# Modulated blocks of an encoder kernel: written in place in their PSUM bank instead of copied to a buffer in SBUF

## Chip, core and metric

The kernel runs on one core of one Trainium2 chip. The metric is the device time of one execution in microseconds. A core has TensorE (PE), VectorE (DVE), ScalarE (ACT), GpSimd (POOL) and SyncE (SP), which run their own instruction streams and wait for each other on semaphores.

## What is computed

Two layers of an encoder run over 1024 prompt rows and 256 sample rows of width 1024. Each layer normalizes its rows, scales and shifts them per channel (the modulation), runs a mixer (latent attention beside a spatial gating group, joined in an output projection), adds the result, normalizes and modulates again and runs a feed-forward part with 2816 hidden channels:

```
h = rmsnorm(x, g_pre_mix) * (1 + sc1) + sh1
x = x + ga1 * rmsnorm(mixer(h), g_post_mix)
h = rmsnorm(x, g_pre_ffn) * (1 + sc2) + sh2
f = (silu(h @ w_gate) * (h @ w_up)) @ w_down
x = x + ga2 * rmsnorm(f, g_post_ffn)
```

The scale and shift columns differ between prompt and sample rows. All inputs and outputs are float32.

## The kernel before

Rows are held as ten tiles of 128 rows, `tokm`. Matrix products run on pairs of values: a high half, rounded to the format that TensorE takes, and a low half, the rest. Each product is three matmuls (`product`, lines 595 to 597): high by low, low by high and high by high. So every input of a product has to be transposed into channel-major order and split into `ht_hi` and `ht_lo`.

One modulated block is one 128-channel slice k of one group of row tiles. A group has 512 or 256 rows in the mixer (`GROUPS`), and 512, 128, 384 or 256 rows in the feed-forward part (`FFN_GROUPS`). There are 112 such blocks. Each goes through this chain:

- TensorE transposes the row tiles of the group, one 128x128 transpose for each, into PSUM bank 6 or 7 (`transposes`, lines 599 to 607). The number n of a block is its place among all users of these two banks, and the bank is 6 + n % 2. Before the transposes TensorE waits until block n - 2 has been read out of the bank: on `s_tbm`, when that block is a modulated one, and otherwise on `s_ht`.
- ScalarE scales and shifts the bank into one of two slots of `tbank` in SBUF (`modulated_bank`, lines 929 to 935). It waits for the transposes and, on `s_ht`, until VectorE is through with block n - 2, whose slot it takes. It then counts `s_tbm` up.
- VectorE waits for `s_tbm`, casts the slot to `ht_hi`, waits for its own cast (`link`), subtracts `ht_hi` from the slot to form `ht_lo`, and counts `s_ht` up (`split_bank`, lines 1351 to 1358).
- TensorE's products of a group wait on `s_ht` until all eight blocks of the group are split.

The same two banks serve the gained blocks (keys "lora" and "out"): there ScalarE writes `ht_hi` from the bank (`gained_bank`, line 947), and VectorE forms `ht_lo` from the bank and `ht_hi` in line 1369.

The order of work is written out by hand and is the same list on every engine: `z_order` for the input products of a layer, `out_order` for the output projection, `AHEAD` and `NEXT_AHEAD` for blocks that are sent ahead within the feed-forward loops. All instructions of an engine run in the order of these lists. Places with modulated blocks are:

- the first run: in layer 0, eight blocks of 512 columns before the first input product;
- pairs of blocks between input products in layer 0, and of the last group in layer 1;
- the start of layer 1: four blocks of 512 columns before its first input product, then four and four blocks of the second group around one product;
- the output projection: two blocks behind each of the products of row tiles 5 to 8, and eight blocks of 128 columns behind tile 8, before the product of tile 9. Behind tiles 5 and 6 gained blocks of the last group follow through the same banks;
- the feed-forward part: eight blocks in a row (four of 384 and four of 256 columns) at the start of its second half, and single blocks or pairs within its loops.

GpSimd splits the weights into `w_hi` and `w_lo` (lines 580 and 582), and SP loads them. Residuals are added on VectorE (lines 1378 and 1380) after ScalarE has formed a sum of squares (line 896). The buffer `tbank` also carries bias rows of the modulation in its first two partitions.

Of the kernel before, what the change touches and what calls it, by code (L numbers as in the profile page):

```python
# [18 lines left out]
F32 = mybir.dt.float32  # L19
F32R = mybir.dt.float32r  # L20
ALU = mybir.AluOpType
ACT = mybir.ActivationFunctionType
AX = mybir.AxisListType

P = 128
# [8 lines left out]
def trunk_program(nc, a, y_prompt, y_sample):  # L34
# [41 lines left out]
    with ctx:  # L76
        ctx.enter_context(nc.allow_non_contiguous_dma(reason="columns of gains, modulation and spatial bias, one element per partition"))

        def sb(name, shape, dt=F32):
            return ctx.enter_context(nc.sbuf_tensor(name, shape, dt))  # L80

        def sem(name):
            return ctx.enter_context(nc.semaphore(name))


        ht_hi = sb("ht_hi", [P, KT, TOK], F32R)
# [8 lines left out]
        tbank = sb("tbank", [P, 2, HB])  # L95
# [9 lines left out]
        ps = ctx.enter_context(nc.psum_tensor("ps", [P, 8, HB], F32))  # L105
# [100 lines left out]
        def w_block(b, kt, n):  # L206
            return [w[:, (b % 2) * HALF_RING:(b % 2) * HALF_RING + kt * n].rearrange("p (k n) -> p k n", n=n) for w in (w_hi, w_lo)]
# [5 lines left out]
        plan, uses, lin, tb_no, tb_keys = {}, [0] * 8, [0], {}, []  # L213
# [181 lines left out]
        s_tbm = sem("bank_modulated")  # L395
        s_ht = sem("ht_ready")
# [61 lines left out]
        def after_product(eng, key):  # L458

            b, n = plan[key]  # L460
            eng.wait_ge(rdy[b], n + 1)
            return b
# [123 lines left out]
        def _(pe):  # L586
            def bank(key):
                b, n = plan[key]
                if n:
                    pe.wait_ge(fre[b], n)  # L590
                return b
# [7 lines left out]
            def transposes(key, srcs):  # L599
                b, n = plan[key][0], tb_no.get(key, 0)  # L600
                if n >= 2:

                    last = tb_keys[n - 2][0]
                    pe.wait_ge(s_tbm if last in ("mix", "ffn") else s_ht, n - 1)
                for i, src in enumerate(srcs):
                    ins = pe.transpose(ps[:, b, i * P:(i + 1) * P], src, ident[:, :])  # L606
                ins.then_inc(rdy[b], 1)
# [7 lines left out]
            for n, key in enumerate(FIRST_MOD):  # L615
                key = ("mod",) + key
                pe.wait_ge(s_wm[n % 2], 32 * (n // 2 + 1))
                b = bank(key)
# [4 lines left out]
            for l in range(L):  # L623

                for e in z_order(l):
                    if e[0] == "tb":
                        _, gi, k = e
                        t0, nt = GROUPS[gi]
                        if k == 0:
                            pe.wait_ge(s_xn, xn_count(l, 0) + t0 + nt)  # L630
                        transposes(("mix", l, gi, k), [row_block(t0 + i, k) for i in range(nt)])
                    else:
                        _, c, t = e
                        n = Z[c][1] - Z[c][0]
                        if c == 0:
                            pe.wait_ge(s_ht, ht_count("mix", l, group_of(t)))
                        b = bank(("z", l, c, t))
                        w = w_block(c, KT, n)
                        for k in range(KT):
                            if t == 0:  # L640
                                pe.wait_ge(s_w, last_piece[(l, c, k)])
                            ins = product(ps[:, b, 0:n], act_cols(t, k), [x[:, k, :] for x in w], k == 0, k == KT - 1)
                        ins.then_inc(rdy[b], 1)

                pe.wait_ge(s_wsl, 16 * (l + 1))
                for i in range(2):
                    transposes(("wsp", l, i), [stage[:, g * P:(g + 1) * P] for g in range(4 * i, 4 * i + 4)])
                pe.wait_ge(s_wsr, 2 * (l + 1))
                for gi, (t0, nt) in enumerate(GROUPS):
                    pe.wait_ge(s_vn, l * NT + t0 + nt)  # L650
                    for bb in range(4):
                        b = bank(("sgu", l, gi, bb))
# [5 lines left out]
                for e in lora_order:  # L658
                    if e[0] == "tb":
                        _, gi, k = e  # L660
                        t0, nt = GROUPS[gi]
# [3 lines left out]
                    else:  # L665
                        t = e[1]
                        pe.wait_ge(s_ht, ht_count("lora", l, group_of(t)))
                        for c in range(4):
                            b = bank(("qkv", l, t, c))
                            blk, kt, k0, n = (4, QKT, 0, H * QK) if c < 2 else (5, KVT, QKT, H * (NOPE + VD))  # L670
                            w = w_block(blk, kt, n)
# [139 lines left out]
                for e in out_order:  # L811
                    if e[0] == "tb":
                        _, gi, k = e
                        t0, nt = GROUPS[gi]
# [7 lines left out]
                    else:  # L822
                        t = e[1]
                        pe.wait_ge(s_ht, ht_count("out", l, group_of(t)))
                        for c in range(2):
                            w = w_block(6 + c, KT, HB)
                            b = bank(("outp", l, t, c))
# [56 lines left out]
        def _(act):  # L884
# [42 lines left out]
                act.dma_start(cols[:, PRE0:PRE0 + KT], a[("g_pre_mix", "g_pre_ffn")[which]][l].rearrange("(k p) -> p k", p=P)).then_inc(s_cols, 16)  # L927

            def modulated_bank(key, groups, gi, scale, shift):
                n = tb_no[key]  # L930
                b = after_product(act, key)
                if n >= 2:
                    act.wait_ge(s_ht, n - 1)
                w = groups[gi][1] * P
                act.activation(tbank[:, n % 2, 0:w], ps[:, b, 0:w], ACT.Identity, bias=shift, scale=scale).then_inc(s_tbm, 1)  # L935

            def modulated_row_bank(key):
                gi, k = key[-2:]
                groups = FFN_GROUPS[key[2]] if key[0] == "ffn" else GROUPS
                g = mod_group(groups[gi][0])  # L940
                modulated_bank(key, groups, gi, c_scale(g, k), c_shift(g, k))
# [51 lines left out]
            for l in range(L):  # L993
# [11 lines left out]
                for n, e in enumerate(z_order(l)):  # L1005
# [6 lines left out]
                    if e[0] == "tb":  # L1012
                        _, gi, k = e
                        g = mod_group(GROUPS[gi][0])
                        modulated_bank(("mix", l, gi, k), GROUPS, gi, c_scale(g, k), c_shift(g, k))
                        continue
                    _, c, t = e
                    b = after_product(act, ("z", l, c, t))
                    if c < 2:
                        n, sq, o = ((QL, QL, ST_Q), (KVR, KVL, ST_KV))[c]  # L1020
# [15 lines left out]
                for i in range(2):  # L1036
                    b = after_product(act, ("wsp", l, i))
# [21 lines left out]
                for e in lora_order:  # L1059
                    if e == ("qkv", TP):  # L1060
                        load_first(0, TP, s_first_prompt)
                    if e[0] == "tb":
                        _, gi, k = e
# [4 lines left out]
                    else:  # L1068
# [5 lines left out]
                        for c in range(2):  # L1074
                            b = after_product(act, ("qkv", l, t, 2 + c))
# [149 lines left out]
                for e in out_order:  # L1225
                    if e[0] == "tb":
                        _, gi, k = e
# [5 lines left out]
                    else:  # L1233
# [12 lines left out]
                        for c in range(2):  # L1246
                            b = after_product(act, ("outp", l, t, c))
# [58 lines left out]
        def _(dve):  # L1306
            chain = [0]

            def link(ins):

                chain[0] += 1
                ins.then_inc(s_dve, 1)
                dve.wait_ge(s_dve, chain[0])
# [19 lines left out]
            for n, key in enumerate(FIRST_MOD):  # L1333
                if n < 2:
                    first_rows(n)
                key = ("mod",) + key
                b = after_product(dve, key)
# [13 lines left out]
            def split_bank(key, groups, gi, k):  # L1351
                n = tb_no[key]
                t0, nt = groups[gi]
                hi, lo = (h[:, k, t0 * P:(t0 + nt) * P] for h in (ht_hi, ht_lo))
                dve.wait_ge(s_tbm, n + 1)
                src = tbank[:, n % 2, 0:nt * P]
                link(dve.tensor_copy(hi, src))  # L1357
                dve.tensor_tensor(lo, src, hi.bitcast(F32), ALU.subtract).then_inc(s_ht, 1)  # L1358

            def split_row_bank(key):  # L1360
                gi, k = key[-2:]
# [43 lines left out]
            for l in range(L):  # L1405
                if l == 0:
                    form_cols(l, 0)
                for n, e in enumerate(z_order(l)):
# [7 lines left out]
                    if e[0] == "tb":  # L1416
                        _, gi, k = e
# [11 lines left out]
                for i in range(2):  # L1429
                    b = plan[("wsp", l, i)][0]  # L1430
                    dve.wait_ge(s_wsh, 2 * l + i + 1)
                    hi, lo = (w[:, 4 * i:4 * i + 4, :].rearrange("p g t -> p (g t)") for w in wsp)
# [59 lines left out]
                for e in lora_order:  # L1492
                    if e[0] == "tb":
                        _, gi, k = e
                        gained_low(("lora", l, gi, k), gi, k, cols[:, GAIN0 + k:GAIN0 + k + 1])
                    else:
# [11 lines left out]
                        for c in range(2):  # L1508
                            b = after_product(dve, ("qkv", l, t, c))
# [120 lines left out]
                for e in out_order:  # L1630
                    if e[0] == "tb":
                        _, gi, k = e
# [110 lines left out]
```

## Time and profile before

| | |
|---|---|
| time, median of 3 runs | 3699.86 us (3693.75 to 3711.45) |
| time of the profiled execution | 3690.44 us |
| span of the profiled execution | 3688.6 us |
| mean granted TensorE clock | 0.958 of 2.4 GHz |
| PE busy | 3356.2 us (91%) |
| DVE busy | 1583.4 us (43%) |
| ACT busy | 1031.6 us (28%) |
| POOL busy | 1396.3 us (38%) |

The span is the time from the first to the last instruction of the core. Busy time counts the instructions of an engine without its waits. All times of single instructions come from this one profiled execution.

### The profile page before, as it was taken

Reading aid. Unit: us, or ns where it says so; the run is one execution under the profiler, and the core shown is the slowest. Engines: PE = TensorE matmul, PEld = TensorE weight load, DVE = VectorE, ACT = ScalarE, POOL = GpSimd, SP = SyncE. Lnnn points to the kernel's source line nnn. Section 1 sums busy time; section 2 is a strip of 40 time slices with the busy share of each in tenths; the row PEclk is TensorE's granted clock in tenths of the full one; section 3 lists DMA queues with packets and bytes.
Section 4 is the critical chain, followed back from the end, with each engine's and each line's share of the span. In section 5 each row is a group of like instructions: output and inputs, shape, how many; then the busy total and the mean of one; then the engine's idle time right before and its main releaser. Section 6 shows DMA issues by size and latency. Waiting matters only on the chain. (4 is left out here: it accounts for less than half of the span.)

```text
span 3688.6 us, 48829 instructions
## 1 busy us (share of the span) xinstructions
PE 3356.2 (91%) x19532; PEld 3022.7 (82%) x19532; DVE 1583.4 (43%) x2807; ACT 1031.6 (28%) x2298; POOL 1396.3 (38%) x804
## 2 busy tenths in 40 slices
PE   5997888888999999899988978887999999999996
PEld 2987777767899998889988767776789999899996
DVE  3115777764333333433333146887333333352223
ACT  2323455553200101210014234777330011121001
POOL 2210577830544454445540302000045444455441
PEclk7998999989999999999999988998999999999998
DMA  6205554432322223322223134111232222233221
GB/s 209 69 20 151 144 157 134 147 100 75 123 78 75 69 80 80 110 80 76 79 68 102 57 113 136 26 38 55 81 120 75 75 75 69 86 120 92 80 75 63
DMA packets 397728, 337.90 MB, mean 92 GB/s; under 512 B 107192, under 2 KB 325000, under 8 KB 397504
## 3 DMA queue, kind: packets, MB, share of 16 engines
q1 hardware_dynamic: 249808, 233.18, 20.7%
q10 hardware_dynamic: 147696, 101.61, 9.4%
q8 instruction: 156, 2.56, 0.3%
q14 instruction: 68, 0.56, 0.0%
HBM read 282.87 MB, written 51.87 MB: 91 GB/s over the span
## 5 line engine op out<-in xcount | busy, mean ns | idle before, releaser
L580 POOL TENSOR_SCALAR w_hi<-raw 128x1024 fp32r<-128x1024 f32 (+2 forms) x400 | 438.1, 1095 | 2183.9 <-PE ps L597 2051.7
L582 POOL TENSOR_TENSOR w_lo<-raw,w_hi 128x1024 fp32r<-128x1024 f32 (+2 forms) x400 | 965.9, 2415 | 33.3
L595 PE MATMUL ps<-ht_lo,w_hi 128*128 128x320 f32 x2816 | 874.1, 310 | 4.9 <-DVE ht_lo L1358 3.0
L596 PE MATMUL ps<-ht_hi,w_lo 128*128 128x320 f32 x2816 | 872.4, 310 | 0.0
L597 PE MATMUL ps<-ht_hi,w_hi 128*128 128x320 f32 x2816 | 872.3, 310 | 0.0
L595 PE MATMUL ps<-w_lo,ht_hi 128*128 128x512 f32 (+2 forms) x2040 | 785.6, 385 | 60.4 <-DVE ht_lo L1358 22.5
L596 PE MATMUL ps<-w_hi,ht_lo 128*128 128x512 f32 (+2 forms) x2040 | 778.5, 382 | 0.0
L597 PE MATMUL ps<-w_hi,ht_hi 128*128 128x512 f32 (+2 forms) x2040 | 777.1, 381 | 0.0
L595 PEld LDWEIGHTS ps<-ht_lo,w_hi 128*128 128x128 f32 x2816 | 530.7, 188 | 8.1 <-DVE ht_lo L1358 3.8
L596 PEld LDWEIGHTS ps<-ht_hi,w_lo 128*128 128x128 f32 x2816 | 530.8, 188 | 1.6
L597 PEld LDWEIGHTS ps<-ht_hi,w_hi 128*128 128x128 f32 x2816 | 530.6, 188 | 0.0
L595 PEld LDWEIGHTS ps<-w_lo,ht_hi 128*128 128x128 f32 x2040 | 393.1, 193 | 130.9 <-DVE ht_lo L1358 24.1
L597 PEld LDWEIGHTS ps<-w_hi,ht_hi 128*128 128x128 f32 x2040 | 392.5, 192 | 65.5
L596 PEld LDWEIGHTS ps<-w_hi,ht_lo 128*128 128x128 f32 x2040 | 393.2, 193 | 61.7
L1667 DVE TENSOR_TENSOR ps<-ps,stage 128x320 f32<-128x320 f32 x176 | 87.8, 499 | 823.1 <-PE ps L597 814.5
L1683 DVE TENSOR_TENSOR tokm<-ps,tokm 128x512 f32<-128x512 f32 x400 | 275.8, 690 | 246.8 <-PE ps L597 246.8
L1271 ACT ACTIVATE stage<-ps 128x320 f32<-128x320 f32 x176 | 75.6, 437 | 924.6 <-PE ps L597 915.9
L1278 ACT ACTIVATE ht_hi<-ps 128x320 fp32r<-128x320 f32 x176 | 77.0, 438 | 560.7 <-DVE ps L1667 560.7
L606 PE MATMUL ps<-ident,tokm 128*128 128x128 f32 x580 | 107.4, 322 | 102.0 <-ACT tbank L935 47.5
L1547 DVE TENSOR_TENSOR ht_lo<-ps,ht_hi 128x512 fp32r<-128x512 f32 (+1 forms) x288 | 177.9, 653 | 37.8 <-ACT ht_hi L1148 36.6
L1536 DVE TENSOR_REDUCE stat<-ps 128x1 f32<-128x1024 f32 (+1 forms) x160 | 169.0, 1056 | 49.4 <-PE ps L597 49.0
L606 PEld LDWEIGHTS ps<-ident,tokm 128*128 128x128 f32 x580 | 78.9, 162 | 127.5 <-ACT tbank L935 36.9
(127 smaller groups left out, 3690.4 us busy)
## 6 DMA issues: line engine op xcount, KB each, us to landing
raw<-in_w_gate_dram SPq DMA_DIRECT2D x88, 512.0 KB, 3.8
raw<-in_w_up_dram SPq DMA_DIRECT2D x88, 512.0 KB, 3.8
raw<-in_w_down_dram SPq DMA_DIRECT2D x88, 512.0 KB, 3.5
raw<-in_w_mod_dram SPq DMA_DIRECT2D x80, 512.0 KB, 4.1
x_rows<-tokm ACTq DMA_DIRECT2D x30, 512.0 KB, 5.0
x_old<-x_rows ACTq DMA_DIRECT2D x30, 512.0 KB, 4.3
kv_rows<-stage ACTq DMA_DIRECT2D x20, 512.0 KB, 3.3
tokm<-kv_rows ACTq DMA_DIRECT2D x30, 320.0 KB, 4.2
```

The costliest lines, as they stand in the source:

```text
L580: pool.tensor_scalar(hi, r, 1.0, 0.0, ALU.mult, ALU.add).then_inc(s_whi, 1)
L582: pool.tensor_tensor(lo, r, hi.bitcast(F32), ALU.subtract).then_inc(s_w, 1)
L595: pe.matmul(out, lhs[0], rhs[1], start=first, stop=False)
L596: pe.matmul(out, lhs[1], rhs[0], start=False, stop=False)
L597: return pe.matmul(out, lhs[0], rhs[0], start=False, stop=last)
L606: ins = pe.transpose(ps[:, b, i * P:(i + 1) * P], src, ident[:, :])
L1271: act.activation(stage[:, c * 320:(c + 1) * 320], ps[:, c, 0:320], ACT.Silu).then_inc(s_sil, 1)
L1278: act.activation(act_ring(half, j % 4)[0][:, c * 320:(c + 1) * 320], ps[:, 2 + c, 0:320], ACT.Copy).then_inc(s_ah, 1)
L1536: link(dve.tensor_reduce(c, psf[:, (u % 2) * 1024:(u % 2) * 1024 + w], AX.X, ALU.max))
L1547: dve.tensor_tensor(lo, ps[:, 4 + c, 0:w * P].rearrange("p (k q) -> p k q", q=P), hi.bitcast(F32), ALU.subtract).then_inc(s_ptl, 1)
L1667: dve.tensor_tensor(up, up, stage[:, c * 320:(c + 1) * 320], ALU.mult).then_inc(s_a32, 1)
L1683: dve.tensor_tensor(f, ps[:, 4 + n % 2, :], f, ALU.add).then_inc(s_acc, 1)
```

## The change

A modulated block is no longer copied to `tbank`. ScalarE reads the bank twice: the first activation writes the high half straight to `ht_hi`, the second writes the scaled and shifted values back into the same bank. VectorE then subtracts `ht_hi` from the bank and writes `ht_lo`; its cast and the wait behind the cast are gone. ScalarE no longer waits for `s_ht`. TensorE waits on `s_ht` for block n - 2 before it writes a bank, whatever kind of block that was.

```diff
             def transposes(key, srcs):
                 b, n = plan[key][0], tb_no.get(key, 0)
                 if n >= 2:
-
-                    last = tb_keys[n - 2][0]
-                    pe.wait_ge(s_tbm if last in ("mix", "ffn") else s_ht, n - 1)
+                    pe.wait_ge(s_ht, n - 1)
...
             def modulated_bank(key, groups, gi, scale, shift):
-                n = tb_no[key]
-                b = after_product(act, key)
-                if n >= 2:
-                    act.wait_ge(s_ht, n - 1)
-                w = groups[gi][1] * P
-                act.activation(tbank[:, n % 2, 0:w], ps[:, b, 0:w], ACT.Identity, bias=shift, scale=scale).then_inc(s_tbm, 1)
+                t0, nt = groups[gi]
+                rows = ps[:, after_product(act, key), 0:nt * P]
+                act.activation(ht_hi[:, key[-1], t0 * P:(t0 + nt) * P], rows, ACT.Identity, bias=shift, scale=scale)
+                act.activation(rows, rows, ACT.Identity, bias=shift, scale=scale).then_inc(s_tbm, 1)
...
                 dve.wait_ge(s_tbm, n + 1)
-                src = tbank[:, n % 2, 0:nt * P]
-                link(dve.tensor_copy(hi, src))
-                dve.tensor_tensor(lo, src, hi.bitcast(F32), ALU.subtract).then_inc(s_ht, 1)
+                dve.tensor_tensor(lo, ps[:, plan[key][0], 0:nt * P], hi.bitcast(F32), ALU.subtract).then_inc(s_ht, 1)
```

## Rows read from the trace of the kernel before

**Rows 1.** The page, part 1: busy time, share of the span, instructions.

```profile
PE 3356.2 (91%) x19532; PEld 3022.7 (82%) x19532; DVE 1583.4 (43%) x2807; ACT 1031.6 (28%) x2298; POOL 1396.3 (38%) x804
```

**Rows 2.** The view of waits: us in total, times, longest us.

```profile
PE ps L606 <- ACT tbank L935: 47.5, 35, 17.1
...
PE ps L595 <- DVE ht_lo L1358: 25.5, 8, 7.3
```

**Rows 3.** Groups by line and form: busy us, mean ns, idle before.

```profile
L935 ACT ACTIVATE tbank<-ps,cols 128x512 f32<-128x512 f32 x48 | 35.7, 775 | 65.1 <-DVE cols L1348 24.2 <-DVE ht_lo L1358 17.5 <-issue 16.4
L935 ACT ACTIVATE tbank<-ps,cols 128x128 f32<-128x128 f32 x16 | 7.3, 457 | 3.9 <-DVE ht_lo L1358 2.6 <-PE ps L606 1.3
L1022 ACT ACTIVATE ps<-ps 128x384 f32<-128x384 f32 x20 | 9.5, 475 | 0.6
L1547 DVE TENSOR_TENSOR ht_lo<-ps,ht_hi 128x512 fp32r<-128x512 f32 x256 | 164.5, 683 | 29.9 <-ACT ht_hi L1148 28.8
```

**Rows 4.** Three lines of VectorE: duration min/median/max in ns, first and last start.

```profile
L1357 DVE CAST ht_hi<-tbank x112: 220/420/2500, 64.7 to 3195.2; 128x512 fp32r<-128x512 f32 x48, 128x256 fp32r<-128x256 f32 x32, 128x128 fp32r<-128x128 f32 x16, 128x384 fp32r<-128x384 f32 x16
L1358 DVE TENSOR_TENSOR ht_lo<-tbank,ht_hi x112: 292/691/2373, 65.2 to 3195.6; 128x512 fp32r<-128x512 f32 x48, 128x256 fp32r<-128x256 f32 x32, 128x128 fp32r<-128x128 f32 x16, 128x384 fp32r<-128x384 f32 x16
L1673 DVE TENSOR_TENSOR ht_lo<-ps,ht_hi x176: 491/492/494, 978.3 to 3645.9; 128x320 fp32r<-128x320 f32 x176
```

**Rows 5.** The timeline, first run: start us, us, instruction, idle before it.

```profile
63.89 1.45 ACT L935 ACTIVATE tbank<-ps,cols 128x512 f32<-128x512 f32 x2 [24.21 <-DVE cols L1348]
65.16 2.18 DVE L1358 TENSOR_TENSOR ht_lo<-tbank,ht_hi 128x512 fp32r<-128x512 f32 x1
68.27 1.12 PE L606 MATMUL ps<-ident,tokm 128*128 128x128 f32 x4 [1.58 <-ACT tbank L935]
83.29 0.69 PE L595 MATMUL ps<-w_lo,ht_hi 128*128 128x384 f32 x1 [3.82 <-DVE ht_lo L1358]
```

**Rows 6.** The timeline, start of layer 1.

```profile
1927.87 1.45 ACT L935 ACTIVATE tbank<-ps,cols 128x512 f32<-128x512 f32 x2 [16.38 <-issue]
1937.33 0.69 PE L595 MATMUL ps<-w_lo,ht_hi 128*128 128x384 f32 x1 [7.31 <-DVE ht_lo L1358]
```

**Rows 7.** The timeline, second token group of layer 1.

```profile
1969.70 1.63 ACT L935 ACTIVATE tbank<-ps,cols 128x512 f32<-128x512 f32 x2 [0.63 <-PE ps L606]
1972.15 0.59 PE L595 MATMUL ps<-w_lo,ht_hi 128*128 128x288 f32 x1
1976.86 1.45 ACT L935 ACTIVATE tbank<-ps,cols 128x512 f32<-128x512 f32 x2
1982.06 0.69 PE L595 MATMUL ps<-w_lo,ht_hi 128*128 128x384 f32 x1 [3.05 <-DVE ht_lo L1358]
```

**Rows 8.** The timeline, last pair of the second token group of layer 0.

```profile
119.01 1.45 ACT L935 ACTIVATE tbank<-ps,cols 128x512 f32<-128x512 f32 x2
122.09 0.44 PE L595 MATMUL ps<-w_lo,ht_hi 128*128 128x384 f32 x1 [3.12 <-DVE ht_lo L1358]
```

**Rows 9.** The timeline, second half of the feed-forward part of layer 0.

```profile
1430.45 1.23 ACT L935 ACTIVATE tbank<-ps,cols 128x384 f32<-128x384 f32 x2 [15.23 <-DVE tokm L1683]
1437.67 0.64 PE L595 MATMUL ps<-ht_lo,w_hi 128*128 128x320 f32 x1 [1.48 <-DVE ht_lo L1358]
```

**Rows 10.** The timeline, output projection of layer 1.

```profile
2657.32 1.45 ACT L935 ACTIVATE tbank<-ps,cols 128x512 f32<-128x512 f32 x2
2660.89 0.41 PE L606 MATMUL ps<-ident,tokm 128*128 128x128 f32 x2 [1.63 <-DVE ht_lo L1369]
...
2693.08 1.28 DVE L1378 SCALAR_TENSOR_TENSOR tokm<-tokm,stat,gate_row 128x1024 f32<-128x1024 f32 x1
...
2704.55 1.45 ACT L935 ACTIVATE tbank<-ps,cols 128x512 f32<-128x512 f32 x2 [2.88 <-DVE gate_row L1387]
...
2710.62 0.45 PE L606 MATMUL ps<-ident,tokm 128*128 128x128 f32 x1 [0.23 <-ACT tbank L935]
```

**Rows 11.** Busy time by stretch: us, PE, PEld, DVE, ACT, POOL busy, PEclk, DMA.

```profile
122.00:127.00 5.00, 4.91 (x19) 4.91 (x20) 0.03 (x1) 0.00 (x0) 0.00 (x0) 0.66 0.02 3
145.00:150.00 5.00, 4.95 (x28) 4.95 (x29) 0.00 (x0) 0.48 (x1) 0.00 (x0) 1.00 0.01 3
```

## The prediction

> **What bounds the kernel now.** I read the page first. TensorE is busy 91% of the span, ScalarE and VectorE far less [rows 1], so work on those two counts only where TensorE stands still for it. The view of waits prices that: TensorE stood 47.5 us in front of transposes until `tbank` was written and 25.5 us in front of products until `ht_lo` was written [rows 2]. The 112 modulated blocks are worth at most these 73 us, 2% of the span. From the timeline I then took each stretch where one of those waits ends last. The 20 blocks sent ahead within the feed-forward loops have their whole chain beside TensorE's work, and I cost them at nothing; their cover is the tiles of gate and up products, and were it gone, one more activation each would cost 20 x 0.67 = 13 us.
>
> **What one block costs before and after.** Before, a 512-column block takes on ScalarE 0.775 us (two in a row 1.45 us, so the second starts 0.67 us after the first) [rows 3, 5], on VectorE a cast (0.42 us) and a subtract (0.69 us; both medians over all sizes) [rows 4]. The same two stretch to 2.5 and 2.37 us at worst [rows 4]; the first run has a subtract of 2.18 us [rows 5], with GpSimd splitting weights beside it.
>
> After, ScalarE issues two activations from one bank. The first has the old one's operands, so it keeps 0.775 us. The second writes the bank in place with pointer scale and bias. The nearest row for a write in place is the square of line 1022, 0.475 us for 384 columns with constant operands; by column it would be about 0.58 us at 512 [rows 3]. I take 0.775 us, since scale and bias are the same kind as in line 935, and keep 0.58 us as the lower end. So a block holds its bank 1.45 us on ScalarE, and ScalarE is free after 1.34 us. VectorE loses the cast and its wait on itself, and the subtract reads the bank: line 1547 does this at 512 columns in 0.683 us [rows 3]. Beside GpSimd: line 1673 has the same operands with a bank as first source and takes 491 to 494 ns in all 176 cases between 978 and 3646 us [rows 4], and GpSimd is busy 38% of the span [rows 1], so many of them stood beside it. So I take 0.69 us, never stretched; upper end 2.2 us.
>
> The Trainium skill speaks against the move here: its page VectorE: DVE Perf Modes, section on the TRN2 errata, charges a VectorE instruction 120 cycles from PSUM and 58 from SBUF, 65 ns more per subtract. The rows above say no such thing (0.683 against 0.691 us). By the page some 33 subtracts on the path would add an estimated 2 us, and the forecast below would be 3710.5 us.
>
> The waits move too. ScalarE no longer waits for `s_ht`; TensorE's next transpose into a bank waits for the subtract of two blocks before instead of the activation. Queued behind that wait stand all of TensorE's later products. A bank's round is now: transposes T, activations 1.45, subtract 0.69, three handovers, for every second block. For a handover I take 0.04 us (the pair of [rows 8] lasts 3.08 us with 3.0 us of instructions in it and five handovers). T is 1.12 us in the first run [rows 5], and about half of that at full clock.
>
> **The sum, place by place.**
>
> First run, layer 0. ScalarE starts at 63.89, products at 83.29 [rows 5]. After: the second block is subtracted at 63.89 + 0.67 x 2 + 1.45 + 0.72 = 67.4; three more rounds of 1.12 + 1.45 + 0.69 + 0.12 = 3.38 end at 77.5. **Gain 5.8 us.**
>
> Start of layer 1, four blocks. Start 1927.87, products at 1937.33 [rows 6]. Second block done at 1931.4, one round of 0.56 + 1.45 + 0.69 + 0.12 = 2.8 more: 1934.2. **Gain 3.1.** The residual work behind it hangs on the next product, and shifts with it.
>
> Layer 1, second token group: four blocks from 1969.70, then a product that began at 1972.15, four blocks from 1976.86, products at 1982.06 [rows 7]. After: the fourth block's transposes wait for the second's subtract, 1969.70 + 2.79 + 0.72 = 1973.2, and end at 1973.8, so the product is 1.65 late. The next four start at 1978.5; second block done at 1982.0, one more round 1984.85. **Loss 2.8.**
>
> Pairs between products. Before, the last pair went from 119.01 to 122.09 [rows 8]; after, 2.79 + 0.72 = 3.5 us instead of 3.1: 0.5 with a small wait for a bank, 0.6. Two more last pairs, of 256 columns, by the same rule 0.4 each. **Loss 1.4.**
>
> Second half of the feed-forward, once a layer: four blocks of 384 columns, four of 256; start 1430.45, products at 1437.67; the pair of 1.23 us gives a step of 0.56 [rows 9]. After: second block done at 1430.45 + 1.12 + 1.23 + 0.6 = 1433.4, a round of 384 columns 2.3, two of 256 columns 1.95 each: 1439.7. **Loss 2.1, twice.**
>
> Output projection, once a layer. Behind the sixth product two modulated blocks and three gained blocks go through the same two banks; the last gained transposes ran at 2660.89 [rows 10]. After: the second subtract ends at 2657.32 + 2.79 + 0.72 = 2660.83, and the gained subtract behind it takes 0.44 more: 0.45 lost; the same behind the seventh. Behind the eighth the residual of line 1378 waited at 2693.08 for the sum of squares that ScalarE runs after two blocks: 1.3 later, and with it the gate row and the blocks at 2704.55 [rows 10]. There two blocks of 512 and eight of 128 columns stand; a 128-column activation is 0.457 us [rows 3], two about 0.82. After: the eighth 512-column block is done at 2705.85 + 2.79 + 0.72 = 2709.4, three rounds of some 1.6 and a transpose end at 2714.6, where the last transpose ended at 2711.07 [rows 10]. So 3.6 with the 1.3. **Loss 4.5, twice.**
>
> Sum: -5.8 - 3.1 + 2.8 + 1.4 + 4.2 + 9.0 = **+8.5 us**. The profiled execution took 3690.44 us (span 3688.6), which makes 3698.9; it lies 9.4 below the median of the runs, 3699.86. Against the median I say **3708.4 us**, 0.23% more. No DMA and no step on SP's or GpSimd's queue is added or moved. With the in-place activation at 0.58 us some 28 rounds on the path each save 0.19 us: 3703.
>
> **The rivals.**
>
> *The clock (slower).* After the 3.12 us gap at 122.09 TensorE was granted 0.66 of 2.4 GHz over 5 us, part of it at 1.2 GHz; after the next shorter gap 1.00 [rows 8, 11]. The first cost 5 x 0.34 = 1.7 us. The losses above lengthen eight gaps: two (256-column ends) would newly fall to 1.2 GHz, six would stay there that much longer. It decides if a gap longer by 0.4 to 3.6 us buys one more such stretch: 8 x 1.7 = 13.6, 3722 us. For it: these gaps all grow. Against: a grown gap may only move the same stretch.
>
> *The subtract from the bank is stretched by GpSimd after all.* Then both gains go: 3717 us. Against it stands line 1673 [rows 4].
>
> *The second activation nearly free (faster).* Were it overlapped with the first, the 28 rounds of 0.67 us fall away: -19, so 3690 us; the sign turns at about 0.37 us each. Against: two successive activations overlap only 0.1 us [rows 3, 5].
>
> *Covered on both sides:* the longer chains meet waits that I did not see, on DMA or on the residuals, and gains and losses mostly vanish: 3700 us.
>
> **Numbers.** About 0.5% (18.5 us) is what a measurement of this kernel can tell from no change. Chances: forecast 0.55, clock 0.20, stretched subtract 0.05, nearly free 0.10, covered 0.10. Of these over 0.5% slower: nearly all of the clock case, half of the stretched one, and a tail of the forecast, 0.23; over 0.5% faster only the far end of the fast case, 0.05; the rest 0.72. The range goes from 3694, inside the fast case with the runs' own scatter, to 3723, which takes in the clock case.
>
> **What would show it.** After, the first run should end near 77.5 us, with no subtract of line 1352 above 0.7 us; ScalarE's in-place activation should read about 0.78 us at 512 columns; the stop before the ninth-tile products of each layer should grow by some 3.6 us, and TensorE's waits in front of transposes should name the subtract, not ScalarE. The forecast is wrong if in-place activations read under 0.4 us, if the subtracts in the first run exceed 1 us, or if the granted clock after these gaps drops clearly further than before.

## The result, and the profile after

The changed kernel takes **3716.66 us** (median, 3706.77 to 3722.09) against 3699.86 us before: a ratio of 1.0042, 95% interval 1.0028 to 1.0056, so 15.5 us slower (10.4 to 20.7). The forecast was 8.5 us more, 3708.4 us: the time lies in its range of 3694 to 3723 us, but the interval leaves 8.5 us out. Line numbers of the kernel after: L930 is the activation into `ht_hi`, L931 the one in place, L1352 the subtract from the bank, L604 the transposes; the products stay in L595 to L597.

Part 1 of the page, after, answers to [rows 1]:

```profile
PE 3369.6 (91%) x19532; PEld 3032.2 (82%) x19532; DVE 1475.8 (40%) x2695; ACT 1089.6 (29%) x2410; POOL 1386.8 (37%) x804
```

VectorE lost 108 us of work and ScalarE gained 58, yet the kernel is slower: neither was the bound. The groups by line and form, after, to be held against [rows 3]:

```profile
L930 ACT ACTIVATE ht_hi<-ps,cols 128x512 fp32r<-128x512 f32 x48 | 37.3, 777 | 53.2 <-DVE cols L1344 23.5 <-issue 16.3 <-DVE gate_row L1381 8.6
...
L931 ACT ACTIVATE ps<-ps,cols 128x512 f32<-128x512 f32 x48 | 35.9, 748 | 0.0
...
L1352 DVE TENSOR_TENSOR ht_lo<-ps,ht_hi 128x512 fp32r<-128x512 f32 x48 | 33.2, 691 | 72.4 <-ACT ps L931 72.4
```

The in-place activation costs 748 ns against 777 for the other: the 0.775 us taken for it was right, the 0.58 us of the lower end was not. The line L1352 over the whole span, min/median/max in ns:

```profile
L1352 DVE TENSOR_TENSOR ht_lo<-ps,ht_hi x112: 291/558/693, 64.2 to 3218.8; 128x512 fp32r<-128x512 f32 x48, 128x256 fp32r<-128x256 f32 x32, 128x128 fp32r<-128x128 f32 x16, 128x384 fp32r<-128x384 f32 x16
```

No subtract takes over 693 ns, where [rows 4] had 2373, and 29 of the 112 had GpSimd at work beside them for nine tenths of their time or more. The Trainium skill's figure (page VectorE: DVE Perf Modes, the TRN2 errata section: 120 cycles from PSUM, 58 from SBUF) would set this subtract an estimated 65 ns above the old one. It takes 691 ns at 512 columns, and in the kernel before the 37 subtracts of that size without GpSimd beside them took 691 to 694, so the measurement does not bear the figure out here. The view of waits, after, answers to [rows 2]:

```profile
PE ps L604 <- DVE ht_lo L1352: 69.7, 46, 17.6
...
PE ps L595 <- DVE ht_lo L1352: 19.0, 8, 3.4
```

TensorE's wait for ScalarE (47.5 us before) is gone, and one for VectorE's subtract of 69.7 us has come; the wait of the products fell from 25.5 to 19.0 us. In sum that is 88.7 against 73.0, of which TensorE's wait for the subtract of gained blocks gives some back (24.0 us before, 16.7 after). The chain moved from two engines that overlapped into one bank that is held until all is done.

The timeline of the first run, after, against [rows 5]:

```profile
62.79 0.78 ACT L930 ACTIVATE ht_hi<-ps,cols 128x512 fp32r<-128x512 f32 x1 [23.52 <-DVE cols L1344]
63.47 0.74 ACT L931 ACTIVATE ps<-ps,cols 128x512 f32<-128x512 f32 x1
64.13 0.78 ACT L930 ACTIVATE ht_hi<-ps,cols 128x512 fp32r<-128x512 f32 x1
64.24 0.69 DVE L1352 TENSOR_TENSOR ht_lo<-ps,ht_hi 128x512 fp32r<-128x512 f32 x1 [1.49 <-ACT ps L931]
...
64.99 1.11 PE L604 MATMUL ps<-ident,tokm 128*128 128x128 f32 x4 [17.59 <-DVE ht_lo L1352]
...
65.58 0.69 DVE L1352 TENSOR_TENSOR ht_lo<-ps,ht_hi 128x512 fp32r<-128x512 f32 x1 [0.65 <-ACT ps L931]
66.14 0.78 ACT L930 ACTIVATE ht_hi<-ps,cols 128x512 fp32r<-128x512 f32 x1 [0.59 <-PE ps L604]
...
76.38 0.69 PE L595 MATMUL ps<-w_lo,ht_hi 128*128 128x384 f32 x1 [2.24 <-DVE ht_lo L1352]
```

The bank of the first block is free for transposes at 64.99, after both activations and the subtract, and ScalarE's third block starts at 66.14: a round of 3.35 us for two blocks, and products 13.59 us after the first activation instead of 19.40. The same shape without GpSimd beside it is the second half of the feed-forward, after, against [rows 9]:

```profile
1435.82 0.67 ACT L930 ACTIVATE ht_hi<-ps,cols 128x384 fp32r<-128x384 f32 x1 [15.22 <-DVE tokm L1677]
...
1438.18 0.56 DVE L1352 TENSOR_TENSOR ht_lo<-ps,ht_hi 128x384 fp32r<-128x384 f32 x1 [0.57 <-ACT ps L931]
...
1439.56 0.56 DVE L1352 TENSOR_TENSOR ht_lo<-ps,ht_hi 128x384 fp32r<-128x384 f32 x1 [0.82 <-ACT ps L931]
...
1440.27 0.66 PE L604 MATMUL ps<-ident,tokm 128*128 128x128 f32 x2 [0.86 <-DVE ht_lo L1352]
...
1440.68 0.56 DVE L1352 TENSOR_TENSOR ht_lo<-ps,ht_hi 128x384 fp32r<-128x384 f32 x1 [0.57 <-ACT ps L931]
...
1443.12 0.42 DVE L1352 TENSOR_TENSOR ht_lo<-ps,ht_hi 128x256 fp32r<-128x256 f32 x1 [0.70 <-ACT ps L931]
...
1445.41 0.42 DVE L1352 TENSOR_TENSOR ht_lo<-ps,ht_hi 128x256 fp32r<-128x256 f32 x1 [0.70 <-ACT ps L931]
...
1445.89 0.63 PE L595 MATMUL ps<-ht_lo,w_hi 128*128 128x320 f32 x1 [1.54 <-DVE ht_lo L1352]
```

Here the products come 10.07 us after the first activation, before 7.22. Measured in the same way in every place (from ScalarE's first activation of the place to the first product that TensorE runs behind the transposes of its last block), in us:

| Place | before | after | difference | forecast |
|---|---|---|---|---|
| first run | 19.40 | 13.59 | -5.81 | -5.8 |
| start of layer 1 | 9.46 | 6.89 | -2.57 | -3.1 |
| second group of layer 1, both halves | 7.65 | 10.73 | +3.08 | +2.8 |
| three last pairs | 7.21 | 8.36 | +1.15 | +1.4 |
| feed-forward second half, layers 0 and 1 | 14.44 | 20.48 | +6.04 | +4.2 |
| output projection: behind the 6th and 7th product, before the last, both layers | 27.33 | 34.79 | +7.46 | +6.4 |
| the residual ahead of its last blocks, both layers | 55.89 | 58.79 | +2.90 | +2.6 |
| sum | | | **+12.25** | **+8.5** |

The 6.4 and 2.6 are the forecast's 4.5 twice, with its 1.3 for the residual apart. The residual's row runs from the start of the eighth product to ScalarE's first block before the last product, and repeats less well than the others: it read 0.35 us longer per layer in a second profile of the kernel before, and 0.7 in a kernel that leaves this part as it was (the first experiment). The measured 12.25 lies inside the interval of 10.4 to 20.7 us. It is good to 1 or 2 us: between the second profiles of the two kernels (experiments 8 and 9) the same sum is 10.8, mostly because the first run of the kernel before took 20.83 us there.

The term that the forecast put at nothing held: from the product behind the last stop of the output projection to the second half of the feed-forward part, the stretch with 16 of the 20 blocks sent ahead, 478.6 and 478.1 us became 479.4 and 478.0.

### The profile page after: what moved, and what is told of

It reads as the page before. It is cut to its first block and busy times, and to the rows that moved or that the text cites. A ratio compares the mean times of both kernels' runs of the same rounds, so it can differ in the third digit from the quotient of the medians.

```text
span 3712.2 us, 48724 instructions
## 1 busy us (share of the span) xinstructions
PE 3369.6 (91%) x19532; PEld 3032.2 (82%) x19532; DVE 1475.8 (40%) x2695; ACT 1089.6 (29%) x2410; POOL 1386.8 (37%) x804
## 5 line engine op out<-in xcount | busy, mean ns | idle before, releaser
L595 PE MATMUL ps<-ht_lo,w_hi 128*128 128x320 f32 x2816 | 873.7, 310 | 5.0 <-DVE ht_lo L1352 3.1
L597 PE MATMUL ps<-ht_hi,w_hi 128*128 128x320 f32 x2816 | 872.0, 310 | 0.0
L595 PE MATMUL ps<-w_lo,ht_hi 128*128 128x512 f32 (+2 forms) x2040 | 789.7, 387 | 54.0 <-DVE ht_lo L1352 16.0
L597 PE MATMUL ps<-w_hi,ht_hi 128*128 128x512 f32 (+2 forms) x2040 | 780.6, 383 | 0.0
L595 PEld LDWEIGHTS ps<-ht_lo,w_hi 128*128 128x128 f32 x2816 | 530.5, 188 | 8.2 <-DVE ht_lo L1352 3.9
L597 PEld LDWEIGHTS ps<-ht_hi,w_hi 128*128 128x128 f32 x2816 | 530.2, 188 | 0.0
L595 PEld LDWEIGHTS ps<-w_lo,ht_hi 128*128 128x128 f32 x2040 | 395.9, 194 | 125.1 <-DVE ht_lo L1352 17.7
L597 PEld LDWEIGHTS ps<-w_hi,ht_hi 128*128 128x128 f32 x2040 | 394.9, 194 | 65.9
L604 PE MATMUL ps<-ident,tokm 128*128 128x128 f32 x580 | 110.9, 328 | 116.8 <-DVE ht_lo L1352 69.7
L604 PEld LDWEIGHTS ps<-ident,tokm 128*128 128x128 f32 x580 | 80.3, 165 | 143.9 <-issue 47.0
```

Source lines behind the costliest of these rows:

```text
L595: pe.matmul(out, lhs[0], rhs[1], start=first, stop=False)
L597: return pe.matmul(out, lhs[0], rhs[0], start=False, stop=last)
```

## The experiments

Theory: the cost is the longer hold of a bank (two activations and the subtract, in series), place by place; the gain is the subtracts no longer stretched by GpSimd; both add up. First rival: the granted clock behind longer gaps is a large part. Second: the loss is not where the chain says.

**1 and 2. The change at the two places that win, and at all others.** In `modulated_bank`, `split_bank` and `transposes`, chosen by key:

```
+ def in_place(key): return key[:3] == ("mix", 0, 0) or key[:3] == ("mix", 1, 0) and key[3] < 4
...
- last = tb_keys[n - 2][0]
- pe.wait_ge(s_tbm if last in ("mix", "ffn") else s_ht, n - 1)
+ last = tb_keys[n - 2]
+ pe.wait_ge(s_tbm if last[0] in ("mix", "ffn") and not in_place(last) else s_ht, n - 1)
```

`modulated_bank` and `split_bank` take the new code where `in_place(key)` holds and the old code elsewhere. The second kernel has `not (...)` in `in_place`.

> The new scheme only for the first run of layer 0 (eight blocks) and the first four blocks of layer 1, the two places where GpSimd splits weights beside the blocks; the old scheme, with tbank, for the other 100 blocks. By the sum of the prediction: 5.8 + 3.1 = 8.9 us less than before, about 3691 us. If the longer time of the whole change comes from the lost clock behind longer gaps, nothing of it is left here, so again 3688 to 3692 us. Rival, that the stretched casts and subtracts cost TensorE nothing in the end because a later wait takes it back: no change, 3700 us.

> The complement: the old scheme at those two places, the new one for the other 100 blocks. By the sum alone 17.4 us more than before, 3717 us. If the places add up and the whole change costs 16.8 us as measured, this must cost 16.8 + 8.9 = 25.7 us, 3726 us. Rival, that the two gains are taken back later: as the whole change, 3717 us, with the first run back at 19.4 us.

Two places: 3691.13 us, ratio 0.9977 (0.9967 to 0.9987), 8.5 us faster; its places sum to 8.5 us less than before, with the residual 7.0. So the gains are not taken back later. The others: 3719.63 us, 1.0060 (1.0045 to 1.0074), 22 us slower (17 to 27); their places sum to 19.1 us more, with the residual 23. The interval holds both 17.4 and 25.7 of the expectation. So the parts add up within it, and the change is two kernels in one: one that wins where GpSimd works beside VectorE, one that loses elsewhere. In the profile before, GpSimd is busy 15.08 of the 19.3 us from 64.0 and 8.81 of the 11.4 us from 1926.0 (the start of layer 1, with casts of up to 2.22 us and subtracts of up to 1.28), and not at all in the other places of the table. That GpSimd does it is shown for the first run (experiment 11); for the start of layer 1 it is read from the profile.

**3. Without the second activation.** The low halves are then formed from a bank without scale and shift.

```
- act.activation(ht_hi[...], rows, ACT.Identity, bias=shift, scale=scale)
+ act.activation(ht_hi[...], rows, ACT.Identity, bias=shift, scale=scale).then_inc(s_tbm, 1)
- act.activation(rows, rows, ACT.Identity, bias=shift, scale=scale).then_inc(s_tbm, 1)
```

> The whole change without its second activation: ScalarE writes only the high half, and VectorE subtracts it from the bank as the transposes left it, so the low halves hold the wrong values and the computation of the scale and shift is left out of them. The moved wait and the subtract from the bank stay. By the chains of the prediction (rounds shorter by 0.67 us at 512 columns): 20 us less than before, 3680 us, and 28 less than the sum for the change. If lost clock is part of the cost, 40 us less than the change as measured, 3677 us. Rival, that the second activation overlaps and the moved wait is what costs: near the change, 3710 to 3717 us.

3680.29 us, 0.9948 (0.9934 to 0.9962). In its waits the subtract keeps TensorE 21 us less than after the change in front of transposes:

```profile
PE ps L604 <- DVE ht_lo L1351: 48.6, 38, 17.1
...
PE ps L595 <- DVE ht_lo L1351: 13.3, 8, 2.2
```

The second activation is worth some 35 us (0.9948 against 1.0042), of which the places and the residual show 29.8. With it left out, 10 of the 15 places measured are shorter than before, and the other five only 0.2 to 0.7 us longer. The time is the 3680 us of the chains; the 3677 us with lost clock lies inside the interval too.

**4. The wait alone, in the kernel before.**

```
- pe.wait_ge(s_tbm if last in ("mix", "ffn") else s_ht, n - 1)
+ pe.wait_ge(s_ht, n - 1)
```

> The kernel before with one part of the change alone: TensorE waits for the subtract of block n - 2 (s_ht) in front of every transpose into a bank, whatever kind of block it was. Then transpose and activation no longer lie beside the cast and subtract of the block two before. By the rounds at the open places (0.4 us for two blocks of 128 columns, 0.4 for 384, 0.5 for 512; none in the two stretched places, where VectorE sets the pace): about 8 us more than before, 3708 us. If lost clock comes on top, up to 3712 us. Rival, that the wait is covered by the transposes' distance: 3700 us.

3711.27 us, 1.0035 (1.0021 to 1.0050), 13 us slower (8 to 18), more than the 8 us expected; its places sum to 12.5, of which 1.2 is the first run's scatter. The view of waits of this kernel:

```profile
PE ps L605 <- DVE ht_lo L1357: 72.8, 46, 20.4
```

That is as much as after the change (69.7), with the old cast, the old buffer and no second activation: in the bank's round the cast and its waits stand where the second activation stands after the change. With one activation and the subtract in the round the whole ran faster than before (experiment 3); with a third step between them, be it the second activation or the cast, it ran slower.

**5. TensorE kept busy in the stops.** The change, with transposes of the identity into a bank that the next product overwrites, between the blocks of the feed-forward second half (shown) and of the last row tile (36, then 4 each). As the fillers of the second half write bank 0, TensorE also waits there until ScalarE has read that bank:

```
+ def warm(b, count):
+     for _ in range(count):
+         pe.transpose(ps[:, b, 0:P], ident[:, :], ident[:, :])
...
+ if gi == k == 0: pe.wait_ge(s_sil, 2 * (tile_no(l, 1, 0) - 1) + 1)
  transpose_ffn(("ffn", l, 1, gi, k))
+ if (gi, k) == (0, 1): warm(0, 12)
+ elif (gi, k) != (0, 0) and (gi, k) != (1, 3): warm(0, 4)
```

> The changed kernel with transposes of the identity put into TensorE's gaps at four places, into a bank that the next product overwrites: the second half of the feed-forward part (12 behind the first two blocks, 4 behind each later one) and the eight blocks of 128 columns before the last row tile of the output projection (36, then 4 each), in both layers. If granted clock lost behind these gaps is part of the cost, transposes and the first products there run at 2.4 GHz: about 12 us less than the change, 3705 us, and some 20 us less at 1.2 GHz in sum. If clock is no part of it, or the fillers do not hold it: 3717 us or a few us more, since fillers can stand in the way of the next transposes.

3703.78 us, 1.0015 (1.0003 to 1.0027), some 10 us less than the change. The rows below give a stretch, its length, TensorE's busy time, the granted clock as a share of 2.4 GHz, and the share and GB/s of transfers. They are the stop of layer 0's second half and the two stretches of 5 us behind it, for the kernel before:

```profile
1430.45:1437.67 7.22, 3.43 (x15) 0.72 0.00 0
```

```profile
1437.70:1442.70 5.00, 5.00 (x19) 0.50 0.61 5
1442.70:1447.70 5.00, 5.00 (x32) 0.88 0.78 165
```

the same for the changed kernel (138.80 is another place, taken up further down):

```profile
1435.80:1445.90 10.10, 3.69 (x15) 0.71 0.00 0
```

```profile
138.80:143.80 5.00, 5.00 (x20) 0.66 0.00 0
1445.90:1450.90 5.00, 5.00 (x21) 0.57 0.59 4
1450.90:1455.90 5.00, 5.00 (x36) 1.00 0.75 132
```

and for the kernel kept busy, the stop in the last line:

```profile
1442.30:1447.30 5.00, 5.00 (x24) 0.66 0.61 5
1447.30:1452.30 5.00, 5.00 (x36) 1.00 0.81 172
1432.70:1442.20 9.50, 6.04 (x45) 1.00 0.01 2
```

Kept busy, TensorE runs the stop at 1.00, and the stop itself is 9.57 us, not 10.07: its pairs of transposes take 0.41 us, not the 0.66 that they took at 0.50, which is 1.2 GHz. Behind it 1.7 us are lost to the lower clock (5 x 0.34), against 2.1 after the change and 3.1 before. So the fillers win back clock that the kernel before was losing too, and not all of the 10 us is a price of the change. What the change adds in clock behind the stops is small: counted in this way over 10 us behind ten of the places, the kernel before loses 18.4 us in each of two profiles, the changed one 19.4 and 20.5.

**6 and 7. Which version is best?** The two-place kernel with such fillers in all four kinds of places, and then with none in the first run and at the start of layer 1. At the ends they are fewer than in experiment 5: 5, then 3 each in the feed-forward half, and 20, then 2 each before the last row tile. The lines that the second of the two kernels lacks:

```
  transposes(("mix", l, gi, k), ...)
...
- if k == 1: warm(bank(("z", l, 0, 0)), 44 if l == 0 else 12)
- elif 1 < k < last: warm(plan[("z", l, 0, 0)][0], 2 if l == 0 else 5)
```

> The kernel of the two places (new scheme in the first run and at the start of layer 1 alone), with such fillers at the same four places and also in those two runs (44 and 12 behind the first two blocks, 2 and 5 behind later ones). Against 3691 us without fillers, if the clock holds: about 4 less in the first run, 2 at the start of layer 1, 6 in the feed-forward halves, 3 in the output projections: 3676 us. If clock is not to be had so: 3691 us or more.

> The kernel of the two places (in-place scheme in the first run and at the start of layer 1 only) with identity transposes between its blocks at the feed-forward second halves and before the last row tile, and none in the first run or at the start of layer 1. If the fillers buy time only where the next products would have run at 1.2 GHz, the stretches behind these stops lose some 1.5 us each in four places and the median is about 6 us below the two-place kernel without fillers, near 3685 us (against 3691). If what they buy is given back in the attention stretch of layer 0, as the profile of the run with fillers everywhere suggests, the median is again 3690 to 3692 us and that stretch reads about 767 us in its profile against 752.

Everywhere: 3690.91 us, 0.9978 (0.9967 to 0.9989), a miss: no better than two places alone. At the ends only: **3683.57 us, 0.9960 (0.9946 to 0.9974)**, the best of the versions that compute the whole, some 30 us under the change (0.9960 against 1.0042). Its stop and the stretches behind it read

```profile
1436.00:1441.00 5.00, 5.00 (x24) 0.66 0.48 7
1441.00:1446.00 5.00, 5.00 (x36) 1.00 0.55 67
1428.70:1435.90 7.20, 4.59 (x34) 1.00 0.00 0
```

as in experiment 5, and its places have the two-place kernel's lengths within 0.2 us but for one of 0.5 (second group of layer 1), so its gain lies behind the stops. There it is seen: the long stretches from three of the four filled stops to the next place are 1.5, 1.5 and 1.6 us shorter than in the two-place kernel, and counted as above the clock loses 13.8 us over the ten places, where the two-place kernel loses 19.6. The two ratios' intervals (0.9946 to 0.9974 and 0.9967 to 0.9987) just touch.

**8 to 10. Second profiles**, of the kernel before, of the change and of the kernel with fillers everywhere, each unchanged.

> The kernel before, unchanged, profiled a second time: how much of a difference between two profiles belongs to the execution. If executions differ in the attention stretches, the time from the last pair of layer 0 to the blocks behind row tile 6 (751.6 us in the first profile) comes out 3 to 10 us longer, the same stretch of layer 1 (639.1 us) 1 to 4 us longer, while each place with modulated blocks repeats within 0.3 us; the span is then 3693 to 3703 us. If the first profile is typical, both stretches repeat within 1 us and the span is 3688 to 3690 us.

> The changed kernel, unchanged, profiled a second time. If the places make the change, each of them repeats within 0.4 us of its first profile (13.6 us the first run, 10.1 us the feed-forward second half, 8.95 us before the last row tile) whatever the span does; the attention stretch of layer 0 (757.3 us) may move by several us. If instead the change itself slows attention (about 6 us more than before), that stretch reads 757 us again and the kernel before repeats its 751.6 us.

> The two-place kernel with fillers in all four kinds of places, profiled a second time. If the 767.3 us of the attention stretch of layer 0 (753.9 without fillers) was that execution's alone, it reads 752 to 760 us and the span is about 3680 us. If the fillers cause it, by sending TensorE into attention at another moment, it reads 765 to 770 us again and the span is about 3692 us.

| us | before | again | change | again | fillers everywhere | again | fillers at the ends |
|---|---|---|---|---|---|---|---|
| first run | 19.40 | 20.83 | 13.59 | 13.60 | 13.13 | 13.09 | 13.60 |
| feed-forward second half, layer 0 | 7.22 | 7.22 | 10.06 | 10.07 | 7.21 | 7.22 | 7.22 |
| last tile, layer 0 | 6.19 | 6.19 | 8.95 | 8.95 | 6.28 | 6.45 | 6.39 |
| attention stretch, layer 0 | 751.6 | 750.9 | 757.3 | 751.9 | 767.3 | 763.6 | 758.4 |
| attention stretch, layer 1 | 639.1 | 641.2 | 641.7 | 645.4 | 641.2 | 642.5 | 640.6 |

An attention stretch runs from the product behind a layer's last pair to the first activation of its output projection's blocks. The places repeat to 0.2 us, but for the first run of the kernel before, where the stretched subtracts vary (two other kernels with the old chain there, experiments 2 and 4, read 20.70 and 20.56), and for the start of layer 1 with fillers everywhere (6.89 and 6.43). The attention stretches do not: they move by 5 us in layer 0 and 4 in layer 1 between two executions of the changed kernel, while of the kernel before only the one of layer 1 moved, by 2, and its span of 3690.6 us lies between the two readings. So the 5.7 us by which attention looked slower after the change is no part of it that these runs can show, though its two stretches together were 5 to 8 us longer than before in both pairs (1398.9 and 1397.3 against 1390.6 and 1392.1). The kernel of experiment 11, which has nothing of the change, reads 1398.0, so such a length does not need it; whether the change adds some of it stays open. With fillers everywhere the stretch of layer 0 is long twice, nearer to the 765 to 770 us of one reading than to the 752 to 760 us of the other; in the two-place kernel without fillers it is 751.8 (one expectation says 753.9). The loss goes with the fillers in the first run and at the start of layer 1, as far as these few profiles show; by what way was not found.

**11. GpSimd moved out of the first run.** The kernel before, whose GpSimd waits with the weights of layer 0 until the blocks are split:

```
+ if i == 0:
+     pool.wait_ge(s_ht, KT)
```

> The kernel before, with GpSimd's first weight split held until the first run's eight blocks are split. If GpSimd's work beside them is what stretches VectorE's casts and subtracts: every cast of the first run near 0.42 us, every subtract near 0.69, and the last subtract about 9.5 us after ScalarE's first activation instead of 19.3; products then wait for weights, so the whole is slower by a few us. If the stretch has another cause (transfers, the cold clock): subtracts of 2.2 us as before.

One run: 3695.22 us. The first run's old chain, from ScalarE's first activation to the last split, for the kernel before, and then for this one (columns: PE, PEld, DVE, ACT, POOL busy, granted clock, share and GB/s of transfers):

```profile
63.90:83.30 19.40, 6.44 (x25) 4.44 (x25) 18.26 (x16) 7.38 (x12) 15.18 (x10) 0.50 0.58 173
```

```profile
62.90:72.70 9.80, 5.41 (x24) 3.84 (x24) 8.57 (x18) 7.36 (x12) 0.00 (x0) 0.67 0.24 76
```

and its first block, last subtract and first product (its lines stand two further down than before):

```profile
64.08 0.43 DVE L1359 CAST ht_hi<-tbank 128x512 fp32r<-128x512 f32 x1 [0.84 <-ACT tbank L937]
...
64.54 0.69 DVE L1360 TENSOR_TENSOR ht_lo<-tbank,ht_hi 128x512 fp32r<-128x512 f32 x1
```

```profile
71.98 0.69 DVE L1360 TENSOR_TENSOR ht_lo<-tbank,ht_hi 128x512 fp32r<-128x512 f32 x1
...
76.03 0.66 PE L597 MATMUL ps<-w_lo,ht_hi 128*128 128x384 f32 x1 [6.03 <-POOL w_lo L584]
```

With GpSimd idle, the cast takes 0.43 us and the subtract 0.69, and VectorE's work on the eight blocks falls from 18.3 to 8.6 us. Transfers fell too (173 to 76 GB/s), as the held GpSimd frees no slot of raw weights, and the mean clock rose (0.50 to 0.67), so this run alone leaves two rivals. The kernel before answers both, in which GpSimd ends its last split of that stretch at 79.49 us:

```profile
78.04 1.45 POOL L582 TENSOR_TENSOR w_lo<-raw,w_hi 128x576 fp32r<-128x576 f32 x1
78.28 1.77 DVE L1358 TENSOR_TENSOR ht_lo<-tbank,ht_hi 128x512 fp32r<-128x512 f32 x1
...
81.48 0.69 DVE L1358 TENSOR_TENSOR ht_lo<-tbank,ht_hi 128x512 fp32r<-128x512 f32 x1
```

The subtract at 81.48 takes 0.69 us at a granted clock of 0.50 with transfers at 371 GB/s; the stretched one of 65.16 had the same clock and 259 GB/s. So neither transfers nor the clock stretch it. The whole old chain then takes 9.4 us (63.27 to 72.67), less than the new one's 13.59. So the new scheme gains in the first run only by keeping out of GpSimd's way. The Trainium skill has this (page SBUF — State Buffer, section Who interferes with whom): a VectorE instruction with two SBUF inputs contends with GpSimd, one with at most one outside the two-port modes does not. The traces agree, with up to 2.37 us before and 0.69 after for the subtract. The expected loss by late weights did not show as one: products waited from 72.67 to 76.03 for them, 12.76 us after the first activation instead of 19.40, and the work up to the next pair took 40.9 us instead of 35.7, so about 1.4 us were left over, which one run can't tell from nothing.

## Why the prediction held, and which terms were too small

**The first run** was forecast as rounds of 3.38 us and a gain of 5.8; it reads 3.35 and 5.81. The round is the mechanism borne out. That the gain agrees to 0.01 us is luck: the old chain's length there varies, and the second profiles make it 7.23. The subtract from the bank was not stretched, so that rival falls. **The second activation** costs 0.748 us where 0.775 was taken, and starts 0.68 us behind the first, so "nearly free" falls too, and experiment 3 gives its price by itself. "Covered on both sides" falls: gains and losses of the places both reach the time (experiments 1 and 2).

The sign, the range and the places held. The size did not: 15.5 us (10.4 to 20.7) were measured for 8.5. The time, 3716.66 us, is nearer to the clock rival's 3722 than to the forecast's 3708.4, and lies in the part of the range that was put there for that rival. As the rival did not come true as priced, it is in part luck that the range held.

**The sum over the places was too small by 3.75 us** (12.25 for 8.5; 2.3 by the second profiles), in four terms of the working:

- *T, the transposes.* The forecast took "1.12 us in the first run, and about half of that at full clock", and used full clock at the start of layer 1. TensorE stands 3.16 us before its first transposes there, which still run at a granted clock of 1.00 and take 0.66 us; the next run at 0.50, which is 1.2 GHz, and take 1.11.

```profile
1937.14 0.66 PE L604 MATMUL ps<-ident,tokm 128*128 128x128 f32 x4 [3.16 <-DVE ht_lo L1352]
...
1938.48 1.11 PE L604 MATMUL ps<-ident,tokm 128*128 128x128 f32 x4 [0.68 <-DVE ht_lo L1352]
```

The round that the forecast counts holds the second of these; its 0.55 us over the forecast's 0.56 are the whole miss there (-2.57 for -3.1).
- *The feed-forward second half*, +2.84 and +3.20 us for 2.1 each (the forecast's own terms add up to 1439.6 and 1.9). By the ends of every second subtract, at 1438.74, 1441.24, 1443.54 and 1445.83, the round of 384 columns takes 2.50 us where 2.3 was taken, and those of 256 take 2.30 and 2.29 where 1.95 was. Part is the clock again (0.5 us of it came back in experiment 5); in layer 1 it fell one block earlier, where three transposes took 0.88 us at 0.50 and not 0.52 at 1.00. Part is the handover to TensorE: 0.04 us was taken, though the pair of [rows 8], 0.08 us over five, gives 0.02; in the first run it is 0.06 (64.24 + 0.69 to 64.99), but here 0.15 (1439.56 + 0.56 to 1440.27).
- *The output projection*, 10.36 us in all for 9.0: rounds of two 128-column blocks take 1.73 us, not 1.6 (ScalarE's starts at 2726.03 and 2727.76, timeline of layer 1, after):

```profile
2721.92 0.78 ACT L930 ACTIVATE ht_hi<-ps,cols 128x512 fp32r<-128x512 f32 x1 [4.06 <-DVE gate_row L1381]
...
2726.03 0.46 ACT L930 ACTIVATE ht_hi<-ps,cols 128x128 fp32r<-128x128 f32 x1 [0.49 <-PE ps L604]
...
2727.76 0.46 ACT L930 ACTIVATE ht_hi<-ps,cols 128x128 fp32r<-128x128 f32 x1 [0.26 <-PE ps L604]
...
2730.87 0.77 PE L595 MATMUL ps<-w_lo,ht_hi 128*128 128x512 f32 x1
```

The 1.3 us for the residual came out at 1.4 to 1.5, with the spread told above.
- *The second group of layer 1* and the pairs: +0.28 and -0.25 us, no matter.

**The clock rival** was priced as one more 1.7 us stretch for each of eight longer gaps, 13.6 us. It does not happen: the stretch at 1.2 GHz behind a gap that grew moves with the gap and hardly lengthens; behind the feed-forward half it even shortens. At the last pair of layer 0 (138.80, 0.66, where [rows 11] have 1.00 in the like place) it seems new, but the second profiles have it the other way round, 1.7 us in the kernel before and none in the change. The clock matters inside the stops, which the forecast left out, and in what fillers win back.

What is left between 12.25 and 15.5 us is inside the interval, and no run tells whether it is anything. The profiled executions stand 22 to 24 us apart (spans 3712.2 twice against 3688.6 and 3690.6), against 15.5 between the medians: both of the kernel before lie 7 to 9 us below its median of 3699.86, both of the changed one 2.7 below its own.

## What to carry to other kernels

The buffer between two engines paid for itself here by freeing its source early: before work is moved back into the bank, count how long the bank is then held (all writers and readers in series) and what TensorE has ready to fill that time with. The same edit can win where a neighbour stretches the old instruction and lose where it does not; apply it by place, and the parts add up. Lengths of stops compare to 0.2 us between two profiles, where no neighbour stretches what runs in them, whole spans to some 10 us, so an effect of a few us is read from the stops.

## What was not expected

Identity transposes in a 7 us stop, doing nothing useful, make the kernel 6 us faster when four such stops are filled (3691.13 to 3683.57, with 1.3 us of it between the two runs of the kernel before). The same fillers in the first run and at the start of layer 1 as well cost that gain again (3690.91), though the mean granted clock of that profile is the higher one, 0.963 against 0.959: a higher clock in the stops is not time by itself.
